# ScalarE's recurrent-block functions grouped by table, first loads in turn, last tile's products on GpSimd

## What is computed

```python
def rg_lru(xc, h0, w_a, b_a, w_x, b_x, lam):
    r = sigmoid(block_diag_linear(xc, w_a, b_a))
    i = sigmoid(block_diag_linear(xc, w_x, b_x))
    log_a = -8.0 * r * softplus(-lam)
    a = exp(log_a)
    bterm = sqrt(-expm1(2.0 * log_a)) * (i * xc)
    ...
    # h_t = a_t h_{t-1} + bterm_t, scanned along time

def lru_mixer(xn, h0, conv_past, w_in, ...):
    gate, xb = split(xn @ w_in)
    xc, conv_tail = causal_dwconv(xb, conv_past, conv_w, conv_b)   # width 4
    h, h_last = rg_lru(xc, h0, ...)
    return (gelu(gate) * h) @ w_out, h_last, conv_tail
```

## Time and profile before

| | before |
|---|---|
| median of 3 runs | 1799.12 us (1798.56 to 1799.45) |
| the profiled execution | 1799.36 us |
| its span on the slowest core | 1797.8 us (the eight: 1794.7 to 1797.8) |
| mean granted TensorE clock | 0.977 to 0.979 of full speed |
| TensorE, VectorE, ScalarE, GpSimd busy | 94%, 67%, 57%, 27% |
| ScalarE's table loads | 168, 1283 ns each |

### The profile page before, as it was taken

One profiled execution on the slowest core, in us unless ns is written; L12 is line 12 of the kernel. 1 busy time (PEld: TensorE's weight loads), 2 busy tenths in 40 slices (PEclk: granted clock), 3 DMA queues, 4 the chain that ended last, 5 costly groups with the idle time before them and its releaser, 6 DMA issues.

```text
span 1797.8 us, 35684 instructions; the slowest of 8 cores (1794.7 to 1797.8 us)
## 1 busy us (share of the span) xinstructions
PE 1694.1 (94%) x11096; PEld 1072.3 (60%) x11096; DVE 1199.7 (67%) x2539; ACT 1024.9 (57%) x1987; POOL 494.3 (27%) x922
## 2 busy tenths in 40 slices
...
## 3 DMA queue, kind: packets, MB, share of 16 engines
...
...
...
## 4 chain that ended last, share of the span: by engine, by line
PE 81%; POOL 5%; DVE 4%; issue 3%; ACT 3%; DMA 3%; DVEq 0%; POOLq 0%; ACTq 0%; SPq 0%
PE PS L570 81%; POOL SB L529 4%; ACT SB L519 2%; DMA SB<-xT 2%; DVE SB L554 2%; DVE SB L529 1%; DMA SB<-lru_w_x_in 1%; ACT L519 1%; DVE SB L545 1%; POOL SB L561 1%; POOL SB L545 0%; DMA yT<-SB 0%; ACT SB L559 0%; ACT PS L519 0%; DVE SB L943 0%
## 5 line engine op out<-in xcount | busy, mean ns | idle before, releaser
L570 PE MATMUL PS<-SB 128*128 128x352 bf16 (+5 forms) x11096 | 1694.1, 314 | 96.0 <-ACT SB L519 44.2
L570 PEld LDWEIGHTS PS<-SB 128*128 128x128 bf16 (+1 forms) x11096 | 1072.3, 98 | 717.5 <-issue 155.6
L529 DVE TENSOR_TENSOR SB<-SB,PS 128x352 bf16<-128x352 f32 (+6 forms) x1112 | 529.8, 511 | 162.0 <-PE PS L570 82.2
L554 DVE SCALAR_TENSOR_TENSOR SB<-SB 128x352 f32<-128x352 f32 (+1 forms) x720 | 370.6, 533 | 272.5 <-ACT SB L559 210.5
L519 ACT ACTIVATE SB<-PS,SB 128x352 f32<-128x352 f32 (+1 forms) x432 | 256.7, 616 | 353.0 <-PE PS L570 350.6
L519 ACT ACTIVATE SB<-SB 128x352 f32<-128x352 f32 (+5 forms) x658 | 312.0, 504 | 189.9 <-DVE SB L554 129.6
L561 POOL COPY SB<-SB 128x2 f32<-128x2 f32 (+2 forms) x472 | 155.5, 334 | 841.6 <-ACT SB L559 686.8
L529 POOL TENSOR_TENSOR SB<-SB 128x352 f32<-128x352 f32 (+6 forms) x267 | 275.4, 1046 | 204.5 <-PE PS L570 64.3
L519 ACT ACT_TABLE_LOAD x168 | 215.5, 1283 | 84.3 <-PE PS L570 55.1
L554 DVE SCALAR_TENSOR_TENSOR SB<-SB,PS 128x352 bf16<-128x352 f32 (+6 forms) x344 | 175.4, 565 | 33.7 <-ACT PS L519 31.8
L559 ACT ACTIVATE SB<-PS 128x352 f32<-128x352 f32 (+6 forms) x408 | 159.7, 409 | 32.9 <-PE PS L570 24.2
...
## 6 DMA issues: line engine op xcount, KB each, us to landing
...
SB<-ple_w_gate POOLq DMA_DIRECT2D x2, 2048.0 KB, 15.5
SB<-gm_w_in POOLq DMA_DIRECT2D x2, 2048.0 KB, 17.4
...
SB<-lru_w_x_in POOLq DMA_DIRECT2D x4, 512.0 KB, 17.1
```

Of the source, the lines that this page charges most:

```text
L529: emit(eng, lambda e: e.tensor_tensor(out=out.ap, in0=a.ap, in1=b.ap, op=op), R=[a, b], W=[out], cost=c)
L554: emit("dve", lambda e: e.scalar_tensor_tensor(out=out.ap, in0=a.ap, scalar=sa, in1=b.ap, op0=op0, op1=op1), R=rr, W=[out], cost=c)
L570: emit("pe", lambda e: e.matmul(ps.ap, lhsT=lhsT.ap, rhs=rhs.ap, start=start, stop=stop), R=[lhsT, rhs], W=[ps], cost=max(0.05, 0.000427 * ...
```

## The change

1. Instructions can be given order-only predecessors. `Prog.order` keeps behind them, in due times too, but no semaphore is waited for. In the recurrent block every Exp of a tile now stands behind the last eight gelus and tanhs, Ln of a norm behind the exps, Sqrt behind exps and norms, and Gelu and Tanh behind the sqrts.
2. The loop is written anew: the norm of the tile after next (from tile 2 on, `ti + 1`) starts at the head of a tile and is finished at the fourth block, half of its squares on ScalarE; sqrt and chain stand at blocks 4 to 7 of the projection; exps follow all gate groups.
3. The first loads wait for each other: the projection's weights for the second quarter of x of tile 0, x of tile 1 for the second weight part (was the fourth), the gate weights for x of tile 1, the output weights for x of tile 2. Vectors and identity go through ScalarE's queue, the vectors first.
4. In the last tile `gate_mult` and every second product of `chain_step` run on GpSimd.

```diff
+            for p in op.order:
+                q = of[p.seq]
+                if q.seq not in nd.preds:
+                    nd.preds[q.seq] = (q, -1.0)
...
-                if at >= 0 and q.eng != "pe":
-                    q.due = min(q.due, nd.due + at - q.dur - q.lat - HOP)
+                if q.eng != "pe" and not (at < 0 and nd.ops[0].is_dma):
+                    q.due = min(q.due, nd.due + max(at, 0.0) - q.dur - q.lat - (HOP if at >= 0 else 0.0))
...
-            act(ps, ps, AF.Ln, bias=epsT.all())
-            act(ps, ps, AF.Exp, scale=-0.5)
+            act(ps, ps, AF.Ln, bias=epsT.all(), order=[] if order is None else order())
+            last = act(ps, ps, AF.Exp, scale=-0.5)
+            if done is not None:
+                done(last)
...
+        load("act", VEC.all(), vecs, K("vec"))
         load_x(0, 4)
-        load("sp", VEC.all(), vecs, K("vec"))
-        load("sp", idf.all(), cst[:, 0:128], K("idf"))
+        load("act", idf.all(), cst[:, 0:128], K("idf"))
         for q in range(4):
-            load("pool", lw_x.v(q), kp(w_lx_in[q], KC), K("lwx%d" % q))
+            load("pool", lw_x.v(q), kp(w_lx_in[q], KC), K("lwx%d" % q), hblock(2, 4, 0, TN) if q == 0 else None)
         load("pool", lw_a.all(), kp(w_la, KC), K("lwa"))
         load("pool", lw_i.all(), kp(w_lx, KC), K("lwi"))
+        load_x(1, 2, lw_x.v(1))
         for q in range(2):
-            load("pool", lw_g.v(q), kp(w_lg_in[q], KC), K("lwg%d" % q))
-        load("pool", lw_o.all(), kp(w_lout, KC), K("lwo"))
-        load_x(1, 2, lw_x.v(3))
+            load("pool", lw_g.v(q), kp(w_lg_in[q], KC), K("lwg%d" % q), hblock(0, 8, TN, TN) if q == 0 else None)
         load_x(2, 2, lw_i.all())
-        load_x(3, 2, lw_g.v(0))
-        load_x(4, 2, lw_g.v(1))
+        load("pool", lw_o.all(), kp(w_lout, KC), K("lwo"), hblock(0, 8, 2 * TN, TN))
+        load_x(3, 2, lw_g.v(1))
+        load_x(4, 2, lw_o.all())
         load_x(5, 2, lw_o.all())
...
+        def keep(name, op):
+
+            PH[name] = (PH[name] + [op])[-8:]
+
+        def phase(*names):
+            return [op for n in names for op in PH[n]]
...
-            act(gg[(ti + 1) % 2][c].v((0, n)), ps, AF.Gelu_apprx_tanh)
+            keep("gelu", act(gg[(ti + 1) % 2][c].v((0, n)), ps, AF.Gelu_apprx_tanh, order=phase("sqrt")))
...
-            act(a, a, AF.Exp, bias=dcol(0, c), scale=dcol(0, c))
+            keep("exp", act(a, a, AF.Exp, bias=dcol(0, c), scale=dcol(0, c), order=phase("gelu", "tanh")))
...
-            act(m, m, AF.Sqrt, bias=0.25, scale=-0.25)
+            keep("sqrt", act(m, m, AF.Sqrt, bias=0.25, scale=-0.25, order=phase("exp", "rstd")))
...
-            tt(b, b, m, ALU.mult)
+            tt(b, b, m, ALU.mult, eng="pool" if ns and c % 2 else "dve")
...
-            tt(gt, gt, a2m[c].v((0, n)), ALU.mult)
+            tt(gt, gt, a2m[c].v((0, n)), ALU.mult, eng="pool" if ns else "dve")
...
+            if 1 < ti:
+                nb = "lru" if ti + 1 < 6 else "xn"
+                gen = lru_norm(ti + 1, ["act", "pool"] * 4) if ti + 1 < 6 else xn_norm(
+                    "nf0", 0, None, ["act", "pool"] * 4, order=lambda: phase("exp"), done=lambda op: keep("rstd", op))
+                bg.append((nb, gen))
...
-                if ti > 0:
-                    if 1 <= c <= 4:
-                        sqrt_step(ti - 1, 2 * c - 2)
-                        sqrt_step(ti - 1, 2 * c - 1)
-                    if c >= 2:
-                        chain_step(ti - 1, c - 2)
...
+                if ti > 0:
+                    if c == 3:
+                        finish("lru")
+                        finish("xn")
+                    if c >= 4:
+                        sqrt_step(ti - 1, 2 * c - 8)
+                        sqrt_step(ti - 1, 2 * c - 7)
+                        chain_step(ti - 1, 2 * c - 8)
+                        chain_step(ti - 1, 2 * c - 7)
...
                     gate_mult(ti - 1, c)
+            for c in range(KC):
                 exp_step(ti, c)
-            if ti > 0 and ti + 2 < 6:
-                bg.append(("lru", lru_norm(ti + 2, "pool")))
-            if ti >= 4:
-                bg.append(("xn", xn_norm("nf0", ti - 4, sqeng="pool")))
```

More of the change, by code:

```diff
@@ L29 @@
 class Op:
-    __slots__ = ("eng", "seq", "fn", "preds", "is_dma", "signal", "ticket", "dbuf", "dval", "cost", "table", "grp", "pos", "lat")
+    __slots__ = ("eng", "seq", "fn", "preds", "is_dma", "signal", "ticket", "dbuf", "dval", "cost", "table", "grp", "pos", "lat", "order")
     def __init__(self, eng, seq, fn, is_dma):
@@ L81, in __init__, with add @@
         self.ngroup = 0
-    def add(self, eng, fn, reads=(), writes=(), dma=False, key=None, cost=0.1, table=None, lat=0.0):
+    def add(self, eng, fn, reads=(), writes=(), dma=False, key=None, cost=0.1, table=None, lat=0.0, order=()):
         op = Op(eng, len(self.all), fn, dma)
@@ L87, in add @@
         op.lat = lat
+        op.order = [x for x in order if x is not None]
         op.grp = self.group if eng == "pe" else None
@@ L489, in s4, with emit @@
             return V(v.ap.rearrange("p (s t) -> p s t", t=4), v.bufs)
-        def emit(eng, fn, R=(), W=(), dma=False, key=None, cost=0.1, table=None, lat=0.0):
-            return P.add(eng, fn, reads=bufs_of(R), writes=bufs_of(W), dma=dma, key=key, cost=cost, table=table, lat=lat)
+        def emit(eng, fn, R=(), W=(), dma=False, key=None, cost=0.1, table=None, lat=0.0, order=()):
+            return P.add(eng, fn, reads=bufs_of(R), writes=bufs_of(W), dma=dma, key=key, cost=cost, table=table, lat=lat,
+                         order=order)
         def width(v):
@@ L504, in build_program, with act @@
                   AF.Ln: frozenset("n"), AF.Sqrt: frozenset("q"), AF.Sigmoid: frozenset("s")}
-        def act(out, in_, func, bias=None, scale=None):
+        def act(out, in_, func, bias=None, scale=None, order=()):
             kw = {}
@@ L518, in act @@
             c = 0.1 + 0.00095 * n + (0.1 if len(rr) > 1 else 0.0)
-            emit("act", lambda e: e.activation(out=out.ap, in_=in_.ap, func=func, **kw), R=rr, W=[out], cost=c, table=TABLES.get(func))
+            return emit("act", lambda e: e.activation(out=out.ap, in_=in_.ap, func=func, **kw), R=rr, W=[out], cost=c,
+                        table=TABLES.get(func), order=order)
         def ew_cost(eng, out, a, b=None):
@@ L740, in finish, with norm @@
                 tick()
-        def norm(c0, n, gname, outs, sqs=None, sqeng="act", after=None, banks=BN):
+        def norm(c0, n, gname, outs, sqs=None, sqeng="act", after=None, banks=BN, order=None, done=None):
             if sqs is None:
@@ L840, in load_part @@
                 load("pool", slot.pproj.all(), kp(w_pp[l], 2), K(slot.name + "d"))
+        PH = {n: [] for n in ("gelu", "exp", "rstd", "sqrt", "tanh")}
+        def keep(name, op):
+            PH[name] = (PH[name] + [op])[-8:]
+        def phase(*names):
+            return [op for n in names for op in PH[n]]
         def lru_norm(ti, sqeng):
@@ L846, in lru_norm, with xn_norm @@
             xn = lxn[ti % 3]
-            return norm(c0, n, "nm0", [xn.v(c, (0, n)) for c in range(KC)], None, sqeng)
-        def xn_norm(gname, ti, sqs=None, sqeng="act"):
+            return norm(c0, n, "nm0", [xn.v(c, (0, n)) for c in range(KC)], None, sqeng,
+                        order=lambda: phase("exp"), done=lambda op: keep("rstd", op))
+        def xn_norm(gname, ti, sqs=None, sqeng="act", **kw):
             c0, npr, ns = TILES[ti]
@@ L853, in xn_norm @@
                 sqs = [s.v((0, n)) for s in sqs]
-            return norm(c0, n, gname, [XN[ti].v(c, (0, n)) for c in range(KC)], sqs, sqeng)
+            return norm(c0, n, gname, [XN[ti].v(c, (0, n)) for c in range(KC)], sqs, sqeng, **kw)
         xcnt = [0]
@@ L910, in ri_group @@
                 mm(psi, lw_i.v(2 * h + kl, (cl * 128, (cl + 1) * 128)), xc[2 * h + kl].v((0, n)), kl == 0, kl == 1)
-            act(av[c].v((0, n)), psr, AF.Tanh, bias=dcol(2, c), scale=0.5)
-            act(thi[c].v((0, n)), psi, AF.Tanh, bias=dcol(3, c), scale=0.5)
+            act(av[c].v((0, n)), psr, AF.Tanh, bias=dcol(2, c), scale=0.5, order=phase("sqrt"))
+            keep("tanh", act(thi[c].v((0, n)), psi, AF.Tanh, bias=dcol(3, c), scale=0.5, order=phase("sqrt")))
             stt(thi[c].v((0, n)), thi[c].v((0, n)), 1.0, xc[c].v((0, n)), ALU.add, ALU.mult)
```

10 lines of the change are left out of this document (4 added, 6 removed).

## The result

The changed kernel took 1782.61 us (median; 1781.71 to 1782.98) against 1799.12: a ratio of 0.9906, 95% interval 0.9891 to 0.9922. That is 16.5 us faster, where 40 were forecast, and 1782.6 lies outside the range of 1742 to 1780. The page is of core 3, the slowest; the shorter timelines further down are of core 5 of the kernel named, where nothing else is said.

What follows compares the result with a forecast made beforehand. TensorE, busy 94% of the span, was taken as the bound, leaving 104 us idle and low-clock matmuls to win. Terms -26 - 8 - 5 + 4 - 5 = -40 took 1799 to 1759 us; 8-in-10 range 1742 to 1780.

Steps and rivals of the forecast that it cites:

- First loads: Start of the kernel: with the loads reordered, tile 1 starts near 46 us instead of 71.6, -26 us (-20 to -30).
- Tile 1: First full tile, no output groups to hide behind: 37 us instead of 45, -8 us (-11 to +2).
- Tiles 2 to 4: Steady tiles: fewer table loads relieve ScalarE, but its work comes in bursts; -5 us in all (-11 to +10).
- The tile followed: One steady tile traced from TensorE's first matmul: ends at 41.4 us instead of 43.8, with 1.5 us idle.
- Tile 5: Tile 5 with the last gates: narrow copies start its burst some 3 us later; 66 us against 62.3, +4 (0 to +8).
- Last tile on GpSimd: First FFN stretch: twelve products taking some 5.5 us leave VectorE, for which TensorE waits; -5 us (-9 to 0).
- The sentence on the shared port: Last tile: by the skill's port locking, the products would return as waiting on VectorE; term near 0 instead of -5.
- Late loads: Rival at the start: x of tile 1 starved behind six weights, or GpSimd held; start gives -12, 1773 us; chance 0.14.
- the 40 us that was to tell: Sign for the start: if x of tile 1 lands after 40 us, the start term is wrong.
- Costly bursts: Rival in the tiles: VectorE's 28 us exposed, tiles at 47 us, tile 1 as before, 1786 us; chance 0.11.
- the slower rival: Rival in the tiles: bursts idle TensorE over 3.5 us per tile, the clock falls, 50.3 per tile; 1803 us; chance 0.05.

## Where the prediction was right and wrong

- **First loads, -26: measured -18.7.** The reading of the starved queue was right: x of tile 1 again lands within 3.3 us behind the sixth weight, and its journey of 14 to 19 us is the forecast's 15.5 to 18. The step that failed is the timing of what comes ahead of it. The quarter that releases the weights was priced with the shortest landing of any x part, though it stands behind another load: the weights are issued at 9.1 to 10.3 and not at 7.6. The sixth then lands at 33.3 to 35.9 and not at 30: on core 5 the first takes 7.5 us from its issue, where 5.4 were allowed, and they follow 3.65 us apart, not 3.4. So x of tile 1 is asked for at 17.6 to 22.4 and not at 16, and its halves land at 33.9 to 36.5 and 36.0 to 38.3, not at 31.5 and 34. That is 3 to 4 us; the other 3 stand behind it, where TensorE comes out of its 8.4 us of idleness with a clock of 0.69 from 39 to 44 us and ScalarE's second four squares wait behind a copy for it. With x in time the start is 45.4, which is the 46 of the forecast, for another reason. TensorE's first projection came at 14.3 to 18.1 and not at 13.5; it waits for x of tile 1 behind that in any case.
- **Tile 1, -8: measured -0.9.** The sum followed ScalarE and gave GpSimd's work no price: the roots wait for GpSimd's clamps, and these for eight squares. With the squares on VectorE it is 38.8, near the forecast's 37. The second error is what made tile 1 slow before: the loads alone bring 38.1 with the table loads kept, so it was the late loads, through 10.5 us of TensorE's waits and a clock of 0.89, and not the table loads.
- **Tiles 2 to 4, -5: measured -3.2.** The size is near, the reason was not, so the hit is luck: the loads alone give 2.6. The tile followed (41.4) is right to 0.3 us for two of the three tiles (41.5, 41.6), the third takes 43.3. But the 43.8 of before was not due to the table loads either.
- **Tile 5, +4: measured +6.0.** Right in sign. The burst made one wait of 3.9 us with the clock falling behind it; without the grouping 2.5 of the 6.0 come back, nearly all by the clock. The other 3.5 are there without any grouping in this tile, and whether the narrow copies make them, as forecast, was not tried.
- **Last tile on GpSimd, -5: measured +0.8.** The term counted products leaving VectorE at no cost to what stays, and they cost 4.0 us there for 3.5 taken away. The sentence on the shared port, kept out of the sum, was the better forecast.
- **The rest:** the later stretches together did not move, as assumed. No rival's price was met by its own mechanism. Late loads (1773) came half true: the start gave 18.7, between their 12 and the forecast's 26, and x landed before the 40 us that was to tell. Costly bursts (1786) is near by its number and wrong by its path: tile 1 did stay as before, but for GpSimd, and none of tiles 2 to 4 took 47. Of the slower rival, the clock that falls behind a long wait appeared in tile 5; in tiles 2 to 4 the waits stay near 1 us.

So 7 of the 24 missing us are the start, 7 tile 1, 2 tile 5, 6 the last tile, 2 tiles 2 to 4.
